# A 31-tap depthwise convolution: one pair of feature tiles goes from VectorE to ScalarE and GpSimd

## What is computed

```python
CONV_WIDTH = 31

def depthwise_conv(x, w):
    k = w.shape[0]
    return lax.conv_general_dilated(
        x, w[:, None, :].astype(x.dtype), window_strides=(1,),
        padding=[((k - 1) // 2, k // 2)], dimension_numbers=('NWC', 'WIO', 'NWC'),
        feature_group_count=x.shape[-1])
```

## Time and profile before

| | us |
|---|---|
| median of 3 runs | 2299.18 (2294.35 to 2299.71) |
| profiled execution | 2293.55 |
| its span | 2291.7 |
| PE busy in the span | 2065.4 (90%) |
| VectorE busy | 859.8 (38%) |
| ScalarE busy | 412.6 (18%) |
| GpSimd busy | 14.5 (1%) |

### The profile page before, as it was taken

The page is one execution under the profiler, slowest core; times in us unless marked ns, Lnnn a source line. Parts: engine busy times, 40 slices in busy tenths (PEclk is TensorE's granted clock), DMA queues, the critical chain, the costliest instruction groups (busy, mean ns, idle before and its releaser), DMA issues. The chain is left out here.

```text
span 2291.7 us, 53982 instructions
## 1 busy us (share of the span) xinstructions
PE 2065.4 (90%) x23610; PEld 1805.2 (79%) x23610; DVE 859.8 (38%) x2334; ACT 412.6 (18%) x1156; POOL 14.5 (1%) x21
## 2 busy tenths in 40 slices
PE   6999967899978766999999999999987998799977
PEld 4668836788867656999999899999977886688855
DVE  3671552678756822010111101111113465225562
ACT  2211441100014122000100000000111035111441
POOL 0000000000000000000000000000000000000000
PEclk7999978999989986999999999999998798888988
DMA  9544002599963121989999898989972321233100
GB/s 389 202 165 189 14 1 74 208 350 337 354 237 111 37 73 63 384 325 364 341 351 354 312 377 319 372 333 351 354 274 105 123 85 74 74 115 125 56 1 19
DMA packets 66943, 480.86 MB, mean 210 GB/s; under 512 B 7312, under 2 KB 8592, under 8 KB 8720
## 3 DMA queue, kind: packets, MB, share of 16 engines
q1 hardware_dynamic: 66704, 477.35, 55.2%
HBM read 476.27 MB, written 1.05 MB: 208 GB/s over the span
## 5 line engine op out<-in xcount | busy, mean ns | idle before, releaser
L1459 PEld LDWEIGHTS PS<-sb_arena,sb_ring 128*64 128x64 f32 x11264 | 478.1, 136 | 9.2 <-issue 5.2
L1459 PE MATMUL PS<-sb_arena,sb_ring 128*64 128x98 f32 x11264 | 483.6, 247 | 1.3 <-ACT sb_arena L1601 0.7
L459 PE MATMUL PS<-sb_U,sb_ring 128*128 128x256 f32 (+1 forms) x1456 | 372.0, 413 | 40.6 <-PEq L206 40.6
L459 PEld LDWEIGHTS PS<-sb_U,sb_ring 128*128 128x128 f32 x1456 | 280.4, 195 | 114.7 <-issue 79.3
L1475 PE MATMUL PS<-sb_arena,sb_ring 128*64 128x98 f32 x5632 | 251.1, 248 | 2.3 <-issue 2.2
L1475 PEld LDWEIGHTS PS<-sb_arena,sb_ring 128*64 128x64 f32 x5632 | 240.2, 137 | 15.6 <-ACT sb_arena L1615 10.9
L1648 DVE TENSOR_TENSOR sb_arena<-PS,sb_arena 128x98 f32<-128x98 f32 x176 | 45.8, 260 | 442.6 <-ACT sb_arena L1590 442.6
L609 PE MATMUL PS<-sb_U,sb_ring 128*128 128x256 f32 x704 | 159.2, 385 | 7.7 <-PEq L206 7.7
L609 PEld LDWEIGHTS PS<-sb_U,sb_ring 128*128 128x128 f32 x704 | 133.9, 193 | 25.9 <-issue 8.1
L383 DVE SCALAR_TENSOR_TENSOR sb_arena<-sb_ring,sb_cs,sb_arena 128x256 f32<-128x256 f32 x280 | 135.8, 485 | 10.0
L459 PE MATMUL PS<-sb_arena 128*64 128x128 f32 (+6 forms) x724 | 124.2, 362 | 11.9 <-DVE sb_arena L1305 11.3
(11 more groups left out here) (286 smaller groups left out, 1775.4 us busy)
## 6 DMA issues: line engine op xcount, KB each, us to landing
sb_ring<-stream SPq DMA_DIRECT2D x450, 1024.0 KB, 6.0
sb_consts<-consts SPq DMA_DIRECT2D x1, 1729.0 KB, 26.1
sb_U<-ctxT SPq DMA_DIRECT2D x1, 1024.0 KB, 6.9
sb_XT<-xT SPq DMA_DIRECT2D x1, 1024.0 KB, 8.7
out<-sb_XT SPq DMA_DIRECT2D x1, 1024.0 KB, 3.8
sb_small<-small SPq DMA_DIRECT2D x1, 292.0 KB, 2.7
sb_consts<-consts SPq DMA_DIRECT2D x1, 129.0 KB, 2.7
sb_all_small<-layer_small SPq DMA_DIRECT2D x1, 110.0 KB, 26.9
```

The lines of the kernel that those rows point to most:

```text
L459: ins = pe.transpose(o, l, r) if t.turn else pe.matmul(o, l, r, start=s, stop=e)
L1459: ins = pe.matmul(PS[c:c + 64, m % 4, h * T:h * T + n], w[:, h, kt, c:c + 64], src[:, kt, 0:n], start=(kt == 0), stop=(kt == KT - 1))
```

## The change

The pair of tiles (2, 3) is taken from VectorE. For each of these two tiles ScalarE makes the first product with the bias straight into `YT` (L1320 of the changed kernel) and then, for each of the other 30 taps, a product into one of four buffers `PR` (L1325); GpSimd adds each product to the tile in `YT` (L1327). A product waits until the addition four before it has freed its buffer, and an addition waits for its product and for the addition two before it, which is the last one on the same tile. The taps are put into the task list in four portions, taps 0 to 7 behind gate 4, 8 to 15 behind gate 5, 16 to 23 behind gate 6, 24 to 30 behind gate 7, each ahead of the diagonals of that m. VectorE's pair (4, 5) moves from behind gate 7 to behind gate 5. `project` learns a third engine, `pool`, with two more semaphores (`chain_p`, `pool_done`), in all six stages that it writes.

```diff
@@ project
-            count = {"act": 0, "dve": 0}
+            count = {"act": 0, "dve": 0, "pool": 0}
...
-            with Stage(nc, name, ["chain_d", "chain_a", "bank_full", "act_done", "dve_done", "acc_ready", "acc_used", "side_done"]) as (
-                    block, (chain_d, chain_a, bank_full, act_done, dve_done, acc_ready, acc_used, side_done)):
-                by = {"act": act_done, "dve": dve_done}
+            with Stage(nc, name, ["chain_d", "chain_a", "chain_p", "bank_full", "act_done", "dve_done", "pool_done", "acc_ready", "acc_used",
+                                  "side_done"]) as (
+                    block, (chain_d, chain_a, chain_p, bank_full, act_done, dve_done, pool_done, acc_ready, acc_used, side_done)):
+                by = {"act": act_done, "dve": dve_done, "pool": pool_done}
...
+                if count["pool"]:
+                    @block.gpsimd
+                    def _(pool):
+                        evacuate(pool, "pool", Chain(pool, chain_p))
@@ the tasks of pw1
+        PR = area(14336, 4 * T).rearrange("p (j t) -> p j t", j=4)
+        added = []
+
+        def taps(k, w):
+
+            x, y = hp[:, k, w:w + T], YT[:, k, :]
+            if w == 0:
+                tasks.append(Task(None, None, "act", lambda act, b, link: nc.scalar.activation(
+                    y, x, ACT.Identity, bias=sm("dw_b", k, 1), scale=dw[:, k, 0:1]), (gated[k],)))
+                return
+            pr = PR[:, len(added) % 4, :]
+            needs = (added[-4],) if len(added) >= 4 else ()
+            tasks.append(Task(None, None, "act", lambda act, b, link: nc.scalar.activation(pr, x, ACT.Copy, scale=dw[:, k, w:w + 1]), needs))
+            needs = (tasks[-1],) + ((added[-2],) if len(added) >= 2 else ())
+            added.append(Task(None, None, "pool", lambda pool, b, link: pool.tensor_tensor(y, y, pr, ALU.add), needs))
+            tasks.append(added[-1])
...
-            if m % 2 and m < 4:
+            if m in (1, 5):
                 tasks.append(convolve_pair(m - 1))
+            if m >= 4:
+                for w in range(8 * (m - 4), min(8 * (m - 4) + 8, W)):
+                    for k in (2, 3):
+                        taps(k, w)
             tasks.append(diagonals(ND + m // 4, 8 * (m % 4), min(8 * (m % 4) + 8, W)))
-        tasks.append(convolve_pair(4))
...
-            return Task(None, matmuls, "act", copy_bias(YT[:, k, :], sm("dw_b", k, 1)), (gated[k], tasks[-2]))
+            return Task(None, matmuls, "act", copy_bias(YT[:, k, :], sm("dw_b", k, 1)), (gated[k], tasks[-1]))
```

## The result

| | before | changed |
|---|---|---|
| median, 6 runs each | 2296.74 us | 2327.20 us |
| profiled execution | 2293.55 us | 2325.77 us |
| its span | 2291.7 us | 2323.9 us |

The ratio is 1.0134, with a 95% interval of 1.0116 to 1.0153: the change costs some 31 us (the two medians lie 30.5 us apart). The forecast was 2331 us, 32.2 more than before.

What follows compares the result with a forecast made beforehand. The `pw1` stage was taken to end 29.3 us after gate 6 and the last diagonal; gate 6, behind VectorE's pair, comes 31.7 us later, plus 0.5 for semaphores: 2299.2 + 32.2 = 2331 us, range 2314 to 2346.

Steps and rivals of the forecast that it cites:

- 1, first addition: In `pw1`, after gates 2 and 3 and ScalarE's first products, GpSimd's first addition starts at about 740.0.
- 5, the last diagonal: On ScalarE in `pw1`, the last diagonal is done at 789.4, before gate 6.
- Step 2: GpSimd's additions come 0.6 us apart with VectorE idle, 0.86 beside it; each takes 0.465 us from VectorE.
- step 3: Portion m = 4: products, eight diagonals, copy, sigmoid and gate 5 let VectorE's pair (4, 5) start at 750.3.
- Step 4: VectorE's pair (4, 5) beside 46 additions takes 24.6 + 21.4 = 46.0 us, ending at 796.3.
- Step 6: Gate 6 reopens PE at 796.9, 31.7 us later; its 28.79 us stay, covered by both starts being cold.
- Step 7: Beside the chain, loads and projection stay unchanged; two more semaphores in six stages cost at most 0.5 us.
- a stage other than `pw1` changes by more than 1 us: Sign that would show the forecast wrong: more than 1 us of change outside the `pw1` stage.
- Rival A: Handover between ScalarE and GpSimd paces additions, from about 1.0 us; 2338.7 at 1.1, 2350 at 1.3; chance 25%.
- Rival B: VectorE's pair isn't stretched and ends at 774.9; ScalarE and GpSimd decide, 16.5 us late, 2316; chance 14%.
- Rival C: Not slower: products come at some 0.27 us, VectorE untouched; PE opens 6.9 us late, 2306; chance 3%.

Runs made afterwards that it cites:

- running sums in PSUM: Changed kernel with VectorE's pairs keeping running sums in a PSUM bank, YT written only by the last tap; ratio 1.0102, PE restart at 89.5 us.
- pair back behind gate 7: Changed kernel with the pair (4, 5) put back behind gate 7, nothing else; ratio 1.0119, PE restart at 90.5 us.
- one column: Changed kernel with GpSimd adding only one of 256 columns, all waits and instructions kept; PE restart at 93.0 us.
- eight buffers: Changed kernel with eight product buffers instead of four, a product waiting for the addition eight before; PE restart at 100.1 us.
- new order, sums in SBUF: Changed kernel with eight product buffers, diagonals ahead of taps, pair (4, 5) in four parts, PE tiles waiting for own diagonals only, sums in SBUF; ratio 1.0008.
- one column and PSUM: Changed kernel with GpSimd adding one of 256 columns and VectorE's running sums in PSUM; PE restart at 78.7 us.
- new order and PSUM: Changed kernel with VectorE sums in PSUM, eight buffers, diagonals ahead of taps, pair (4, 5) in four parts, PE tiles waiting for own diagonals only; ratio 0.9943.

## Why the prediction was right, and where its terms were off

The mechanism was the one named: PE waited for gate 6, gate 6 for the pair, the pair for gate 5 and for 46 additions. Term by term, from the first matmul of `pw1` (the forecast's times less 696.43):

| step | forecast | measured |
|---|---|---|
| 1, first addition | 43.6 | 44.0 |
| 2, pace with VectorE idle | 0.6 | (9.64 - 0.73) / 13 = 0.69 |
| 2, pace beside VectorE | 0.86 | 757.33 - 756.47 = 0.86 |
| 3, the pair starts | 53.9 | 55.1 |
| 4, the pair takes | 46.0 | 750.58 + 44.65 - 749.19 = 46.0 |
| 5, the last diagonal | 93.0 | 94.4 |
| 6, PE restarts | 100.5 | 101.7 |
| 6, PE's two tiles take | 28.8 | 29.5 |

- *Step 2* was low by 0.09 us with VectorE idle, and the ten additions that set the end of portion m = 4 make 0.9 us of it. The whole error of step 3, 1.2 us, goes through to the restart: 33.0 us late instead of 31.7. ScalarE's products are 0.51 us long and some 0.40 apart, not the 0.31 of the earlier trace rows. From the first biased product to the first addition it took 1.57 us (738.06 - 736.49) instead of 0.9, but ScalarE began 0.3 us sooner, since tile 2 needs gate 2 only: the start moved by 0.4 us. Nothing behind it moved, since GpSimd is slower.
- *Step 4* was exact to 0.1 us: the pair ran from 55.1 to 101.1. The price of 0.465 us came from four additions in the earlier trace rows and held for 46.
- *Step 6*, PE's own time: I said the longer rest costs nothing. PE's two tiles took 29.52 us instead of 28.79, and the granted clock shows why. Windows of 2 us counted from the restart, the second and the third, first of the kernel before, then of the changed one (window, busy time of PE, matmuls, granted clock, DMA):

```profile
767.19:769.19 2.00, 2.00 (x7) 0.61 0.00 0
769.19:771.19 2.00, 2.00 (x11) 1.00 0.00 0
...
797.80:799.80 2.00, 2.00 (x7) 0.50 0.00 0
799.80:801.80 2.00, 2.00 (x8) 0.74 0.00 0
```

 The clock stood at 0.50 (1.2 GHz) for 3.6 us behind the restart before and for 5.1 in the changed kernel, then at 1.00 (2.4 GHz). A microsecond at half the clock costs half a microsecond, and with that taken off every kernel's tiles take 27.0 us, all but the same. The time at 0.50 is worked out from the mean granted clock in windows of 1 us:

| kernel | rest | at 0.50 | tiles take | less half of that |
|---|---|---|---|---|
| before | 11.3 | 3.6 | 28.79 | 27.0 |
| changed | 44.1 | 5.1 | 29.52 | 27.0 |
| running sums in PSUM | 31.9 | 3.6 | 28.78 | 27.0 |
| pair back behind gate 7 | 32.9 | 6.0 | 29.99 | 27.0 |
| one column | 35.4 | 3.5 | 28.74 | 27.0 |
| eight buffers | 42.5 | 3.2 | 28.60 | 27.0 |
| new order, sums in SBUF | 5.0 | 3.2 | 28.59 | 27.0 |
| one column and PSUM | 21.1 | 4.1 | 29.06 | 27.0 |
| new order and PSUM | none | 0 | 26.94 | 26.9 |

 So the cover in step 6 was wrong in one way: both starts are cold, but a cold start isn't always the same length. It doesn't follow the length of the rest (3.2 us at half clock after 5.0 and after 42.5 us); what sets it stays open.
- *Step 7*: two more semaphores cost not 0.09 us a stage but 0.14, if the longer gap is theirs; no run took them out alone. Between the last copy of `pw2` and ScalarE's next work there were 1.09 us, and 1.23 now:

```profile
875.69 2.56 ACT L306 ACTIVATE sb_arena<-sb_arena 128x256 f32<-128x256 f32 x8 [1.23 <-PEq L206]
```

 At the end of `pw1` the gap grew by 0.15 (1.62 to 1.77). If it is so in all six stages, that is 0.8 us instead of 0.5.

The sum of the stage is thus 133.0 - 99.2 = 33.8 us in the traces, where I had 31.7: 1.2 from the start of the pair, 0.7 from the clock, 0.14 from the gap. The spans differ by 32.2, as forecast to the tenth, and that is luck: the second execution came to the stage 2.3 us sooner. The medians differ by 30.5 us. The forecast is 3.8 us high, and 2.4 of that is the median of before, 2299.18 of three runs and 2296.74 of six. The sign "a stage other than `pw1` changes by more than 1 us" was seen and meant nothing: the 1.7 us near 191 us lie in matmuls that the change leaves as they were, and the slower time was there again in another changed kernel.

Two sums of the rivals are slightly off, with no weight here: C's 2306 leaves out step 7 and would be 2306.6, just over the 0.3%, and A at 1.25 us gives 2347, not 2346.

Rival A needed a pace of 1.0 us or more; it was 0.69 and 0.86, and PE waited for VectorE. The one column and the eight buffers speak against it too. Rival B's case was made by putting the sums in PSUM: the restart is then 20.7 us late (89.5 against 68.8), where I had 16.5. The pace again: 44 additions lie on that chain (10, 12, 12 and 10), and 44 x 0.09 is 4.0 us. Rival C needed products at 0.27 us; they came at 0.40 at best, and even with additions of one column and no stretch the restart is 10 us late.

## What to carry to other kernels

In this kernel work moved to GpSimd was not off VectorE while VectorE read two inputs from SBUF. Price each moved instruction by what it takes from VectorE (here 0.465 us for an addition that replaced a multiply-add of 0.40), and if that is a loss, first put one of VectorE's inputs in PSUM. When an engine with a list order gets slow work, look at what stands behind it in the list: here gates and diagonals that another engine waited for made 32.5 us of difference, and the work moved, with its order put right, some 7. A consumer should wait for the pieces that it reads, not for the last of all.

## What the runs showed of the hardware

- A multiply-add with its sum in PSUM runs at 0.39 us apart, as fast as from SBUF (0.40), and leaves GpSimd at 0.69.
- GpSimd's addition of 128 x 256 follows its neighbour after 0.69 us when VectorE is idle or does multiply-adds with one input in SBUF, and after 0.86 beside multiply-adds with two; the one of 128 x 1 takes 0.19.
- VectorE's multiply with bias (one tensor input) was stretched too while it wrote SBUF, 1.46 us for two instead of 0.74, and not while it wrote PSUM (0.99 for two in both places).
- After a rest, PE's granted clock stood at 0.50 for 3.2 to 6.0 us in eight restarts, with no relation to rests of 5 to 44 us; the 124 matmuls took 27.0 us plus half of that time.
- Taking turns is not assured: a GpSimd addition of one column was held for 15.27 us, while 38 or so multiply-adds (15.27 / 0.40) went by. The Trainium skill, SBUF — State Buffer, section "Who interferes with whom", calls the shared ports an exclusive lock on which the second instruction blocks; this one was held through a whole row of instructions, not through one. It was seen once.
